# A dense attention stage in which V is loaded as weights and the turned probabilities are streamed

## What is computed

```python
proj = h @ w_in                                   # h: RMS-normed x
qb = rms_norm(qb.reshape(b, l, 4, 3, 64), qn_b)   # 4 groups of 3 query heads
kb = rms_norm(kb.reshape(b, l, 4, 64), kn_b)      # one key and value head each
s = einsum('bqhgd,bkhd->bhgqk', axial(q), axial(k)) * 64 ** -0.5
p = softmax(s, axis=-1)
ob = einsum('bhgqk,bkhd->bqhgd', p, v)
```

## Time and profile before

| | |
|---|---|
| median of 3 runs | 3942.34 us (3941.73 to 3945.46) |
| profiled execution | 3943.24 us |
| its span | 3941.4 us |
| TensorE busy | 3807.1 us, 97% |
| VectorE busy | 2627.4 us, 67% |
| ScalarE busy | 2114.4 us, 54% |
| POOL busy | 908.2 us, 23% |
| phase "b" | 0 to 677.9 us of the span |

### The profile page before, as it was taken

The page is one execution under the profiler, slowest core; times in us unless marked ns, Lnnn a source line. Parts: engine busy times, 40 slices in busy tenths (PEclk is TensorE's granted clock), DMA queues, the critical chain, the costliest instruction groups (busy, mean ns, idle before and its releaser), DMA issues. The chain is left out here.

```text
span 3941.4 us, 70807 instructions
## 1 busy us (share of the span) xinstructions
PE 3807.1 (97%) x24938; PEld 3573.8 (91%) x24938; DVE 2627.4 (67%) x5374; ACT 2114.4 (54%) x3855; POOL 908.2 (23%) x1387
## 2 busy tenths in 40 slices
PE   8999999999999989999999999999997999999998
PEld 7989989999997779999999989999887999999998
DVE  6565665666664677777777757777527777777775
ACT  6554545555552255655565546555423556555654
POOL 5132230333331111111111133332121111111222
PEclk9999999999989989999999999999998999999999
DMA  3000001122124388887888731000335888778874
GB/s 110 9 23 7 24 15 38 41 73 60 54 81 159 121 254 254 264 249 240 254 264 249 244 101 51 32 23 16 139 138 173 257 252 270 246 238 253 270 246 134
DMA packets 492026, 583.96 MB, mean 148 GB/s; under 512 B 21536, under 2 KB 447520, under 8 KB 491808
## 3 DMA queue, kind: packets, MB, share of 16 engines
q1 hardware_dynamic: 473952, 522.44, 41.3%
q0 software_dynamic: 15680, 50.34, 5.5%
q10 hardware_dynamic: 2176, 8.39, 0.6%
HBM read 514.89 MB, written 66.22 MB: 147 GB/s over the span
## 5 line engine op out<-in xcount | busy, mean ns | idle before, releaser
L1814 DVE TENSOR_TENSOR wl<-raw,wh 128x2048 fp32r<-128x2048 f32 x382 | 871.7, 2289 | 185.2 <-ACT wh L1757 178.9
L1757 ACT CAST wh<-raw 128x2048 fp32r<-128x2048 f32 x384 | 730.5, 1911 | 34.5 <-DMA raw<-in_w_gate 26.9
L1935 PE MATMUL ps_g<-xT,wh 128*128 128x384 f32 x2048 | 593.6, 356 | 0.0
L1935 PE MATMUL ps_u<-xT,wh 128*128 128x384 f32 x2048 | 593.5, 356 | 0.0
L1937 PE MATMUL ps_g<-xT,wl 128*128 128x192 f32 x2048 | 477.3, 253 | 0.0
L1937 PE MATMUL ps_u<-xT,wl 128*128 128x192 f32 x2048 | 477.2, 253 | 0.0
L151 PE MATMUL psP<-ring_high,hTh 128*128 128x384 f32 (+1 forms) x1344 | 461.5, 343 | 11.1 <-DVE ring_low L826 4.9
L153 PE MATMUL psP<-ring_high,hTl 128*128 128x384 f32 (+1 forms) x1344 | 442.7, 329 | 0.0
L152 PE MATMUL psP<-ring_low,hTh 128*128 128x384 f32 (+1 forms) x1344 | 442.5, 329 | 0.0
L1080 PEld LDWEIGHTS psO<-V,pT 128*128 128x128 f32 x3456 | 419.2, 193 | 20.5 <-issue 10.5
L1080 PE MATMUL psO<-V,pT 128*128 128x64 f32 x3456 | 417.3, 273 | 5.1 <-ACT pT L759 3.3
(11 more groups left out here) (228 smaller groups left out, 7785.0 us busy)
## 6 DMA issues: line engine op xcount, KB each, us to landing
raw<-in_w_gate SPq DMA_DIRECT2D x128, 1024.0 KB, 6.2
raw<-in_w_up SPq DMA_DIRECT2D x128, 1024.0 KB, 5.9
raw<-in_w_down SPq DMA_DIRECT2D x128, 1024.0 KB, 8.3
xb<-in_x SPq DMA_DIRECT2D x72, 256.0 KB, 2.8
out_y<-yb SPq DMA_DIRECT2D x24, 512.0 KB, 2.6
h_rows<-hb SPq DMA_DIRECT2D x24, 512.0 KB, 2.9
ring_raw<-in_w_a SPq DMA_DIRECT2D x24, 384.0 KB, 4.0
xb<-in_x SPq DMA_DIRECT2D x12, 512.0 KB, 4.3
```

The costliest lines, as they stand in the source:

```text
L1757: act.copy(wh[:, j % SPL], raw[:, j % RAW]).then_inc(w_high, 1)
L1814: dve.tensor_tensor(wl[:, j % SPL], raw[:, j % RAW], wh[:, j % SPL].bitcast(F32), ALU.subtract)\
L1935: both = lambda **fl: pe.matmul(ps[:, f, 0:2 * CAP], wh[:, j % SPL, k, fs], xT[:, k].rearrange("p h c -> p (h c)"), **fl)
```

## The change

The product with V is turned round. V is kept as float32r in a high and a low part (`V` has 2 x 64 columns) and is loaded as the weights; the turned probabilities, also in a high and a low part (`pT` has 2 x 128 columns for each block), are streamed. A matmul then gives 128 rows (64 dimensions by the high part of V, 64 by the low) and 256 columns (128 queries by the high part, 128 by the low). `join` (VectorE) adds the two column halves, O (`turn_output`, TensorE) turns the result, `add_halves` (VectorE) adds the two row halves, and `divide` (ScalarE) multiplies by the reciprocal. The copies of turned probabilities are all on ScalarE, and VectorE makes the low part of each (`turned_low`). V's low part is made by POOL.

The list of events becomes, in the steady state, `R u, V(u-1, second batch), S u+2, [T], O u-1, V(u, first batch)`; O takes a room of `psT` too. The maximum of unit u+2 is issued on VectorE after the `add_halves` of u-1. `HELD` goes from 4 to 5, `pT` gets 3 slots. T of tile p-2 stands between the two halves of projection p; the last tiles of a turn, and those projected between units, are turned on their own, the latter three units after their projection. All four W of a turn stand behind its first four units, none inside a projection. For tiles projected between units, the products with the cosines go from VectorE to POOL. `SCALE` goes into the gains, the maximum is negated by its own instruction, and places of x go from 4 to 3 and into the space of `qT`; the rotation table is loaded in a shorter form by four DMAs.

```diff
-RING, LAG, HELD = 6, 5, 4
+RING, LAG, HELD, SLOTS = 6, 5, 5, 3
...
-            if self.dense and p and p % NT == 0 and half == 0:
-                got += [("W", p // NT * WQ + 2), ("W", p // NT * WQ + 3)]
+            if half == 0 and between is not None:
+                got.append(("T", between))
...
-                if x < 2 and (self.follows or not last):
+                if x < (2 if last else WQ) and (self.follows or not last):
                     plan.append(("W", (i + 1) * WQ + x))
...
+            if kind == "U" and n:
+                events += [("R", n), ("V", n - 1, 1)]
+            elif kind == "U":
+                events.append(("R", n))
             if kind == "P":
-                turn_up_to(n - 2)
-                events.extend(self.projection(n, self.norm_of.get((0, n + 2)) if n < NT else None))
+                turn_up_to(n - 3)
+                between = n - 2 if n >= 2 and turned == n - 3 else None
+                events.extend(self.projection(n, self.norm_of.get((0, n + 2)) if n < NT else None, between))
+                turned = max(turned, n - 2)
                 since[n] = 0
             elif kind == "U":
-                events.append(("R", n))
                 if n + 2 < len(self.units):
                     turn_up_to(self.units[n + 2][3])
                     events.append(("S", n + 2))
-                if turned + 1 in since and since[turned + 1] >= 1:
+                if turned + 1 in since and (since[turned + 1] >= 3 or turned + 2 in since):
                     turn_up_to(turned + 1)
                 for p in since:
                     since[p] += 1
-                events.append(("V", n))
+                if n:
+                    events.append(("O", n - 1))
+                events.append(("V", n, 0))
...
-    XH = {"b": 4, "a": 2, "c": 3}[name]
+    XH = {"b": 3, "a": 2, "c": 3}[name]
...
+                if dense and between_units(p):
+                    wait_alone(pool, squared, p + 1, tally)
+                    turned_x = xr[:, b, :].rearrange("p (h c) -> p h c", c=HD)
+                    for c0 in range(0, HD, R1):
+                        cs = rope[:, NT if c0 >= 2 * R1 else t, 0:R1]
+                        ins = pool.tensor_tensor(turned_x[:, :, c0:c0 + R1], x[:, :, c0:c0 + R1], spread(cs, 1, nh), ALU.mult)
...
+                if dense:
+                    pool.tensor_tensor(V[:, t, HD:], v32[:, b, :], V[:, t, 0:HD].bitcast(F32), ALU.subtract).then_inc(v_split, 1)
...
-                act.mul(V[:, t, :], psP[:, nh * HD:NC], rt[:, steps[s]["order"], t:t + 1]).then_inc(evacuated, 1)
+                if dense:
+                    if p >= 2:
+                        act.wait_ge(v_split, p - 1)
+                    act.mul(v32[:, b, :], psP[:, nh * HD:NC], rt[:, 0, t:t + 1])
+                act.mul(V[:, t, 0:nkv * HD], psP[:, nh * HD:NC], rt[:, steps[s]["order"], t:t + 1]).then_inc(evacuated, 1)
...
+            def divide(u):
+
+                segs = units[u][1]
+                act.wait_ge(rden_ready, u + 1)
+                act.wait_ge(o_added, u + 1)
+                for c, (h, t, *_) in enumerate(segs):
+                    out = osb[:, (units[u][0] * NT + t) % OR, h]
+                    ins = act.mul(out, out, rden[:, u % 4, c:c + 1])
+                ins.then_inc(o_done, 1)
...
+                if dense:
+                    dve.tensor_reduce(nbias[:, r, hs], psS[:, u % 2, :].rearrange("p (c k) -> p c k", c=ns)[:, :, 0:w],
+                                      AX.X, ALU.max, negate=True).then_inc(max_ready, 1)
+                    return
...
+            def turned_low(u, k):
+                slot = work.spot(u, k)[0]
+                dve.wait_ge(pT_act, batch0[u] + k + 1)
+                dve.tensor_tensor(pT[:, slot, :, 1, :], room_of("R", u, k).rearrange("p (x c) -> p x c", c=P),
+                                  pT[:, slot, :, 0, :].bitcast(F32), ALU.subtract).then_inc(pT_dve, 1)
+
+            def join(u):
+
+                segs = units[u][1]
+                dve.wait_ge(pv_done, batch0[u] + 2)
+                if u >= 2:
+                    dve.wait_ge(o_turned, u - 1)
+                for c in range(len(segs)):
+                    ins = dve.tensor_reduce(oT[:, u % 2, c * P:(c + 1) * P], o_half(u, c).rearrange("p (f c) -> p c f", f=2),
+                                            AX.X, ALU.add)
+                ins.then_inc(o_summed, 1)
+
+            def add_halves(u):
...
+                dve.reciprocal(rden[:, u % 4, 0:ns], den[:, u % 4, 0:ns]).then_inc(rden_ready, 1)
...
+                dve.wait_ge(o_turned, u + 1)
+                dve.tensor_reduce(osb[:, p % OR:p % OR + ns, h],
+                                  room_of("O", u)[:, 0:ns * P].rearrange("p (n f c) -> p n c f", f=2, c=HD),
+                                  AX.X, ALU.add).then_inc(o_added, 1)
...
-                if e[0] == "R":
+                if e[0] == "R" and dense:
+                    turned_low(e[1], 0)
+                    if e[1]:
+                        join(e[1] - 1)
+                    turned_low(e[1], 1)
+                elif e[0] == "R":
                     copies(e[1])
...
+            def weigh_batch(u, k):
...
+                for x, (c, j) in enumerate(units[u][2][k]):
+                    k0, nk = segs[c][2:4]
+                    ins = pe.matmul(o_half(u, c), V[:, k0 + j, :], pT[:, slot, x, :, :].rearrange("p f c -> p (f c)"),
+                                    start=(j == 0), stop=(j == nk - 1))
+                ins.then_inc(pv_done, 1)
+
+            def turn_output(u):
+                pe.wait_ge(o_summed, u + 1)
+                room_free(("O", u))
+                for c in range(len(units[u][1])):
+                    ins = pe.transpose(room_of("O", u)[:, c * P:(c + 1) * P], oT[:, u % 2, c * P:(c + 1) * P], ident)
+                ins.then_inc(o_turned, 1)
```

More of the change, by code:

```diff
@@ L264, in unit, with projection @@
         self.units.append((i, segs, batches, need))
-    def projection(self, p, norm):
+    def projection(self, p, norm, between=None):
         got = []
@@ L328, in dense_order @@
             for x, tile in enumerate(tiles):
-                at = [(j + 1) * free // len(tiles) for j in range(len(tiles))]
+                at = [((j + 1) * free + len(tiles) // 2) // len(tiles) for j in range(len(tiles))]
                 plan += lead[(at[x - 1] if x else 0):at[x]] + [tile]
@@ L371, in dense_order @@
                 events.append((kind, n))
-        return events
+        return events + [("V", len(self.units) - 1, 1), ("O", len(self.units) - 1)]
     def by_act(self, u, k):
-        return k == 0 or (self.dense and u % 2 == 1)
+        return k == 0
     def count_batches(self):
@@ L454, in attention_phase @@
     gains = ph.sb("gains", [P, NS, nh * HD])
-    rope = ph.sb("rope", [P, NS, NT, 2, W])
+    rope = ph.sb("rope", [P, NT + 1, 3 * R1] if dense else [P, NS, NT, 2, W])
     half = ph.sb("half", [P, nh])
-    xb = ph.sb("xb", [P, XH, HC])
+    if not dense:
+        xb = ph.sb("xb", [P, XH, HC])
     ssx = ph.sb("ssx", [P, 2, 2])
@@ L525, in weights, with between_units, x_half, o_half @@
         return steps[i // turns]["w"][i % turns].rearrange("p (q k c) -> q p k c", q=WQ, c=NC)[q % WQ]
+    def between_units(p):
+        return p >= NT and p % NT < PT
+    def x_half(x):
+        return x_places[x % XH][:, :] if dense else xb[:, x % XH]
+    def o_half(u, c):
+        return psO[:, c * 2 * P:c * 2 * P + 2 * P] if len(units[u][1]) > 1 else psO[:, u % 2 * 2 * P:u % 2 * 2 * P + 2 * P]
     def raw_quarter(q):
@@ L727, in high @@
                 act.wait_ge(turned, p + 1)
+                if dense and p == NT - HC // P:
+                    act.wait_ge(x_squared, 2 * len(work.norms))
                 act.copy(qT[:, 0:2 * pairs, tile_cols(p)].rearrange("p (a b) c -> p a b c", b=2),
@@ L916, in output @@
                 p = i * NT + t
[L917 to L921 removed]
+                if p >= OR:
+                    dve.wait_ge(stored[p % OR], 16 * (p // OR))
                 dve.wait_ge(pv_done, batch0[groups[g][-1] + 1])
@@ L963, in _ @@
                     maximum(e[1])
-                    if dense:
-                        tile_up_to(2)
+                if e[0] == "O":
+                    if e[1] == UT - 1:
+                        join(e[1])
+                    add_halves(e[1])
                 if e[0] == "T":
@@ L974, in _ @@
                     tile_up_to(3)
-                    tile, stage = e[1], 0
+                    tile, stage, age = e[1], 0, 0
                     if not dense:
@@ L979, in _ @@
                     weight_low(e[1])
-                if e[0] == "V":
+                if e[0] == "V" and dense:
+                    if e[2] == 0:
+                        maxima()
+                        tile_up_to(age + 1)
+                        age = min(age + 1, 2)
+                elif e[0] == "V":
                     output(e[1])
-                    if dense:
-                        tile_up_to(3)
                 if e[0] == "OL":
```

156 lines of the change are left out of this document (113 added, 43 removed).

## The result

| | before | changed |
|---|---|---|
| median | 3942.31 us (3941.73 to 3945.46, 4 runs) | 3979.36 us (3975.88 to 3985.64, 4 runs) |
| ratio | | 1.0097, 95% interval 1.0084 to 1.0109 |
| profiled execution, its span | 3943.2, 3941.4 us | 3978.1, 3975.9 us |
| first matmul of the next stage | 677.93 us | 709.52 us |

The change costs 37 us by the medians; the forecast was 3952 us, 8.7 over the profiled execution before and 9.7 over the median. Of the 34.5 us that the span grew, 31.6 arise before the next stage starts. The first matmul of that stage is the better measure for what follows: from the first matmul of the experts of layer 0 to the end, work that is the same everywhere, the profiled executions of this study took from 2534.1 us (run 11) to 2541.6 (run 5), and 2534.7 before.

The account below looks back on a forecast made before the run. TensorE, running without a gap, was taken to bound the kernel before. Against 3943.2 us, -64.8 + 11.3 (units of two segments) + 17.0 + 15.2 + 6.0 + 16.5 + 7.2 + 1.5 - 1.2 = +8.7 gave 3952 us, range 3908 to 3980.

Parts of the forecast that it names:

- turned tiles among units: Units holding a turned tile: next transposes wait for its bank, 1.68 us against 0.83 before; 20 x 0.85 = 17.0 us added.
- the splits: Sixteen weight splits issued behind units delay the next unit's copies and first subtraction by 1.15 us each; 16.5 us added.
- projections back to back: Evacuations in projection stretches go from 4.54 to 5.1 us apart; 2.4 us in each of three stretches, 7.2 us added.
- The unit: Plain unit of attention work: pitch falls from 3.54 to 3.00 us, saving 120 x 0.54 = 64.8 us.
- the ring: Plain unit: transposes, copy, subtraction, sum, second subtraction, then the next transposes, which need the freed PSUM bank; 2.95 us.
- no overlap on VectorE: Rival: new VectorE instructions start only when the last has ended; unit 3.46 us, 55 us more, 4007 us; chance 0.05.
- a product that is no cheaper: Rival: each f32r matmul costs its weight load, 0.19 instead of 0.116 us; TensorE's unit 3.43, total 4004 us; chance 0.04.
- dearer reduces: Rival: reduces cost by run, or a step is late; 0.15 us more per unit, 18 us, 3970 us; chance 0.12.
- Tile steps on VectorE: Sum, rotation and scaling, once hidden by TensorE: 1.26 us for each of 12 tiles, 15.2 us; last tiles of turns 6.0.
- End of the stage, start: Stage end: join, turn, add and divide in a row add 1.5 us; the start was put at 0.
- clock: Rival: TensorE's clock falls in 16 turned-tile units at some 1.7 us each; 27 us more, 3979 us; chance 0.06.
- Cover holds: Rival: tile steps and splits fall into VectorE's waiting time and cost nothing; 38 us less, 3914 us; chance 0.28.

Follow-up runs that it names:

- run 11: Changed kernel with, in the stretches of projections, the turned tile issued ahead of the projection instead of between its halves: 3973.38 us, ratio 1.0074.
- run 5: Changed kernel with HELD back from 5 to 4, so two units instead of one stand among a turn's eight tiles: 3986.33 us, ratio 1.0112.
- run 7: Changed kernel with the maximum reading only the first half of each segment's scores, leaving out half of its work: 3971.15 us, ratio 1.0069.
- run 9: Changed kernel with certain tiles turned one unit earlier and, on VectorE, rotation and scaling of a turn's last tile in one unit: 3973.2 us, ratio 1.0076.
- run 6: Changed kernel with low parts of weight splits beside units on GpSimd instead of VectorE, and ScalarE's half ahead of the division: 3967.27 us, ratio 1.0064.
- run 10: Changed kernel with the edits of run 9 and run 6 together: 3953.48 us, ratio 1.0025.
- run 2: Changed kernel with two of each turn's four weight splits moved back inside the next turn's first projection: 3983.88 us, ratio 1.0107.
- run 4: Changed kernel plus matmuls of the identity into an unused part of a PSUM bank where TensorE waits longest: 3980.59 us, ratio 1.0097.
- run 14: Run 10 plus the first three tiles projected among a turn's units turned inside the next projection, not in their own unit: 3942.69 us, ratio 1.0003.
- run 15: Run 14 plus the edit of run 11: 3934.02 us against 3940.7 for the kernel before, ratio 0.9984.
- run 12: Changed kernel plus matmuls on constants only in TensorE's longest waits, 12 behind a split, 10 between a turned tile and its scores: 3996.28 us, ratio 1.0136.

## Why the prediction was right in direction and wrong in size

The direction, slower, and the structure held: a unit that pays, and steps beside it that are no longer covered. The step that failed is the term for turned tiles among units, 20 x 0.85 = 17.0: it put the wait behind a tile at 1.68 us wherever the tile stood, and left out the seven places where a tile is turned directly ahead of the scores that need it. They cost 16.7 us more. The terms for the splits and for projections back to back were too small as well, and one that was too dear hid a third of it. By the prediction's own steps:

- **The unit: right.** 3.05 us against 3.00. The ring was put at 2.95, VectorE's own sum at 2.98, and VectorE named as last. Run 7 shows that it is the ring, at 3.05: from the transposes to ScalarE's copy and from VectorE back to TensorE it takes 0.66 and 0.14 us, not 0.64 and 0.05. 120 x 0.05 = 6 us. Units of two segments cost 0.48 more than plain ones, 0.47 forecast. The rival "no overlap on VectorE" fell: 655.46 lies 0.08 us before the end of the reduce at 655.13. With it fell, for these instructions, what the Trainium skill, "VectorE: DVE Perf Modes", section "The DRAIN you can't avoid", says of the next instruction and the pipe. The rivals of a product that is no cheaper and of dearer reduces fell too. But four matmuls on V take 0.56 us, 0.14 apart, where 0.116 was taken: the product is 1.12 us and not 0.93, which stays hidden only because the ring is longer still.
- **Turned tiles among units: mis-sized, the largest error.** The term took 1.68 us for every tile. In the rests it is 1.86. Where the tile stands directly ahead of its own scores in an opening it is 3.6 to 4.3 (8.49 - 4.89, 9.23 - 4.89, 8.87 - 4.89, 7.44 - 3.53), with a fall of the clock in it. At the ends of turns the last two units take 10.87, 9.51 and 11.09, against 7.96 with a tile of the rests. The four openings cost 9.1 more than taken and the three ends 7.6 more than a tile of the rests, 16.7 in all. Both follow from the rule `since >= 3` in the diff, since the seventh unit of a turn needs the last tile; the event list had to be written out to see it, and I reasoned about a typical unit instead. Run 9 gave 12.7 back by order alone, the waits and the falls of the clock behind them together.
- **Weight splits: right in kind, too small.** 1.15 us forecast per split, 1.36 and 1.61 measured: 12 x 1.36 + 4 x 1.61 = 22.8 against 16.5. Runs 6 and 10 confirm the term (12.4 alone, 16.4 on top of run 9). That no place was free for them, run 2 shows.
- **Projections back to back: the step was right, the comparison wrong.** 5.1 us forecast, 5.07 measured. But the eight tiles took 38.9 us before and after, once with two units among them and once with one: (38.89 - 2 x 3.54) / 7 = 4.54 before, (38.91 - 3.05) / 7 = 5.12 now, 4.05 per turn instead of 2.4. And in the first turn, put at 0, the unit is missing just the same: 3.5 us. Together 8.5 more.
- **Tile steps on VectorE: too dear.** 1.26 per tile forecast, 0.20 + 0.33 measured; the last tiles' rotation 0.4 instead of 1.5. Since the ring binds and not VectorE, small steps find some 0.07 us in each unit (3.05 against VectorE's 2.98), and the sum after a projection is free. 13 us less than forecast, which hid part of the error.
- **End of the stage, start:** 2.4 us better and 1.0 worse than taken.

Summed: 6 + 1.6 (tiles in the rests) + 16.7 + 6.3 + 8.5 - 13.2 - 2.4 + 1.0 = 24.5, for 22.9 missing in the stage: 1.6 too much, as far as this reckoning goes. Behind the stage the span grew by another 2.9 us, 2.1 of them between the first matmul of the next stage and that of the experts (728.8 us before, 730.9 changed), which the prediction put at nothing; by the medians it is 5.4.

The **clock** was a rival of its own with 27 us for 16 falls. There were ten behind the start, at 1.3 to 1.6 each (run 4), and they come behind waits that have another cause: when run 9 took the waits away, the time at the lower clock fell from 48 to 21 us. "Cover holds" fell at the sixteen splits and was half right for the tile steps.

What stays open: why, by the medians, what follows the stage takes 5 us more in the changed kernel than before, 7 to 11 more in runs 9, 10, 14 and 15, and less than 1 in run 11; and how much of the openings' cost is clock. In the unit shown it is 0.9 us on the scores and the transpose behind them. The sum of it would need kernels in which only the clock differs; runs 4 and 12 changed the waits as well.

## What to carry to other kernels

When an engine stops being full, everything that lay in its shadow has to be priced again, and not for a typical unit: write out the order of events and look for the places where a producer stands directly ahead of its consumer, for there the whole chain is exposed. Name the ring that sets the pitch by what it contains; an engine at 99% may be beside it, and only shortening one of its instructions tells (run 7). A change that costs time as a whole may hold a part that pays: here 1% slower became 0.16% faster, with five moves in the order and one change of engine.

## What the hardware showed that was not expected

- Two of VectorE's steps with both inputs in SBUF stretch from 0.48 to 0.94 and from 0.42 to 0.55 us beside GpSimd's instructions; those that read PSUM do not (run 6).
- Each filler matmul of 128 columns on plain float32 constants ran as two passes, so 12 of them lasted 2.8 us (run 12).
- The two subtractions and the reduces overlap by 0.08 us although each writes rounded output or reduces over runs of two elements.
- From the experts of layer 0 to the end, with the same work, the profiled executions differ by up to 7.5 us between kernels that differ only in the first stage.
